# In the second attention, the turns straight behind the scores and the gates parts behind the turns

## The reference, cut to what matters

```python
o_a = diff_attention(qa, ka, va, ...)        # 4 heads, two softmaxes each
o_b = nsa_attention(qb, kvb, ...)            # 8 heads: compressed, selected, window
merged = (jax.nn.sigmoid(gate_a) * (o_a @ w_branch_a[l])
          + jax.nn.sigmoid(gate_b) * (o_b @ w_branch_b[l]))
h = h + merged @ w_out[l]
```

## Time and profile before

| | us |
|---|---|
| median of 3 runs (2418.17 to 2419.32) | 2419.19 |
| the profiled execution | 2417.22 |
| its span, first to last instruction | 2415.5 |
| TensorE busy (97% of the span) | 2351.6 |
| VectorE busy (73%) | 1771.4 |
| ScalarE busy (46%) | 1119.5 |
| GpSimd busy (57%) | 1370.9 |

### The profile page before, as it was taken

How to read it: one execution, slowest core, us unless ns; L and a number is a source line. 1 busy time by engine, 2 the same in 40 slices (tenths; PEclk the granted TensorE clock), 3 DMA queues, 4 the chain that set the end, 5 groups by cost and what they waited for, 6 DMA issues and landing times.

```text
span 2415.5 us, 32822 instructions
## 1 busy us (share of the span) xinstructions
PE 2351.6 (97%) x11991; PEld 1993.6 (83%) x11991; DVE 1771.4 (73%) x2989; ACT 1119.5 (46%) x2163; POOL 1370.9 (57%) x698
## 2 busy tenths in 40 slices
PE   8999999999999999999999999999998999999998
PEld 7866888888886666887889899999998888888887
DVE  4986684253237766655899869999963699999998
ACT  4355322223224555335544368888863333333333
POOL 3423454554432212443535767777777788889885
PEclk9999999999999999999999999999999999999999
DMA  4201222222521111323224578999999799999995
GB/s 160 87 18 37 104 87 91 100 98 84 187 71 54 53 36 36 122 90 107 83 85 156 190 231 310 355 349 353 352 359 396 288 373 376 366 356 366 361 357 211
DMA packets 152500, 476.60 MB, mean 197 GB/s; under 512 B 14768, under 2 KB 47920, under 8 KB 142000
## 3 DMA queue, kind: packets, MB, share of 16 engines
q1 hardware_dynamic: 115504, 340.69, 39.1%
q0 software_dynamic: 36864, 134.23, 15.3%
HBM read 422.44 MB, written 52.43 MB: 197 GB/s over the span
## 4 chain that ended last, share of the span: by engine, by line
PE 87%; DVE 5%; DMA 3%; ACT 2%; POOL 2%; issue 1%; SPq 0%; ACTq 0%; DVEq 0%; POOLq 0%
PE bank_pair L2394 22%; PE bank_pair L286 17%; PE bank_pair L288 17%; PE bank_pair L287 17%; PE bank_pair L2363 2%; DMA u_raw<-expert_u 2%; PE bank_pair L775 1%; PE bank_pair L1448 1%; PE bank_pair L1485 1%; POOL u_lo L2068 1%; PE bank_pair L1501 1%; PE bank_pair L297 1%; PE bank_pair L1457 1%; PE bank_pair L298 1%; DVE stage L2539 1%
## 5 line engine op out<-in xcount | busy, mean ns | idle before, releaser
L255 POOL TENSOR_TENSOR w_lo<-w_raw,w_hi 128x2048 fp32r<-128x2048 f32 (+3 forms) x94 | 408.9, 4350 | 573.2 <-ACT w_hi L250 573.2
L2068 POOL TENSOR_TENSOR u_lo<-u_raw,u_hi 128x1024 fp32r<-128x1024 f32 x128 | 317.9, 2484 | 182.2 <-ACT u_hi L2064 181.5
L286 PE MATMUL bank_pair<-uh,u_lo 128*128 128x384 f32 x1024 | 348.1, 340 | 17.0 <-POOL u_lo L2068 16.5
L288 PE MATMUL bank_pair<-uh,u_hi 128*128 128x384 f32 x1024 | 344.8, 337 | 0.0
L287 PE MATMUL bank_pair<-ul,u_hi 128*128 128x384 f32 x1024 | 344.8, 337 | 0.0
L2124 POOL TENSOR_TENSOR v_lo<-v_raw,v_hi 128x1024 fp32r<-128x1024 f32 x128 | 309.4, 2417 | 43.9 <-ACT v_hi L2120 42.7
L250 ACT ACTIVATE w_hi<-w_raw 128x2048 fp32r<-128x2048 f32 (+3 forms) x95 | 171.5, 1805 | 287.9 <-PE bank_pair L288 280.1
L2588 DVE TENSOR_TENSOR h_raw<-h_raw,g_in 128x384 f32<-128x384 f32 x128 | 272.7, 2131 | 30.7 <-DMA h_raw<-h_scratch 30.7
L2120 ACT ACTIVATE v_hi<-v_raw 128x1024 fp32r<-128x1024 f32 x128 | 135.8, 1061 | 300.3 <-PE bank_pair L2394 243.4
L286 PE MATMUL bank_pair<-xh,w_lo 128*128 128x512 f32 x624 | 245.8, 394 | 5.2 <-DVE sig L1737 2.1
L288 PE MATMUL bank_pair<-xh,w_hi 128*128 128x512 f32 x624 | 243.7, 390 | 0.0
(11 more groups left out here) (458 smaller groups left out, 5226.4 us busy)
## 6 DMA issues: line engine op xcount, KB each, us to landing
w_raw<-w_small SPq DMA_DIRECT2D x77, 1024.0 KB, 4.8
u_raw<-expert_u SPq DMA_DIRECT2D x128, 512.0 KB, 6.1
v_raw<-expert_v SPq DMA_DIRECT2D x128, 512.0 KB, 7.4
h_scratch<-h_act SPq DMA_DIRECT2D x128, 192.0 KB, 4.3
g_scratch<-stage SPq DMA_DIRECT2D x24, 1024.0 KB, 8.8
g_in<-g_scratch SPq DMA_DIRECT2D x16, 1536.0 KB, 11.5
h_raw<-h_scratch SPq DMA_DIRECT2D x128, 192.0 KB, 6.3
w_raw<-w_small SPq DMA_DIRECT2D x8, 768.0 KB, 4.2
```

Source lines behind the costliest of these rows:

```text
L255: pool.tensor_tensor(wl[g % 2][:, :n], raw[g % 2][:, :n], wh[g % 2][:, :n].bitcast(F32), ALU.subtract).then_inc(sem("lo_done"), 1)
L286: pe.matmul(out, al, bh, start=(k == 0), stop=False)
L288: last = pe.matmul(out, ah, bh, start=False, stop=(k == len(pairs) - 1))
L2068: pool.tensor_tensor(u_lo[c % 2][:, :, :], u_raw[c % 4][:, :, :], u_hi[c % 2][:, :, :].bitcast(F32), ALU.subtract)\
```

## The change

Only the order within TensorE's steps changes. The first part of a step no longer stands between the scores and the turns: the turns come straight behind the scores (in steps 1 and 2 the turned compressed weights too), and all parts of the step stand behind the turns and ahead of the values. No instruction, wait or buffer is added or removed, and the streams of the other engines are the same.

```diff
             for s in range(NU + 3):
                 if s < NU:
                     if s >= 2:
                         scores(s)
-                    gates_part(gates_parts(s)[0])
                 if s in (1, 2):
                     compressed_turned(s - 1)
                 if 2 <= s <= NU + 1:
                     transposes(s - 2)
                 if s < NU:
-                    for q in gates_parts(s)[1:]:
+                    for q in gates_parts(s):
                         gates_part(q)
                 if s >= 3:
                     values(s - 3)
```

## The result

The changed kernel takes 2432.13 us (median of 5 runs, 2429.81 to 2436.36) beside 2418.96 of the kernel before on the same chip: ratio 1.0059, 95% interval 1.0045 to 1.0072. The forecast was 2431.3, slower by over 0.2%. The profiled execution, the slowest of the five, took 2436.36, with a span of 2434.6: 19.1 us more than the one before. From L1514 on every line of the new kernel has a number one lower (`weights` ends in L1716 and L1722, `maxima` are L1700 and L1704).

The account below looks back on a forecast made before the run. VectorE was busiest in steps 0 to 16, TensorE full from 816 to 916 us. Terms 2.1 + 0.85 + 3.8 + 5.4 = 12.1 us, added to the median 2419.19, gave 2431.3 us, 0.5% slower, range 2423 to 2436.

Parts of the forecast that it names:

- the signs that were named: Profile after: turns wait on L1254 six times, L1723 some 4 us, other steps' scores-to-scores distance unchanged, TensorE below 100 us.
- The fourth: Sign in the profile after: VectorE's L1723 lasts some 4 us in steps 25, 33 and 41.
- the first steps of the later heads: Steps 24, 28 to 44: turns wait for ScalarE's copy, a part falls behind them; 0.69 and 0.58 alternating, 3.8 us.
- steps 16 to 20: Step 19's turns wait for ScalarE's copy, a part falls behind: 0.69, some 0.15 in step 20; together 0.85 us.
- steps 5, 9 and 13: Turns wait for VectorE's weights, the part now follows them and delays the next scores: 3 x 0.69 = 2.1 us.
- The hold: Steps 25, 33, 41: L1723, now later, waits until POOL's L255 ends, delaying the next turns; 1.8 us each, 5.4.
- The estimate of 0.2 more a time: L1721, ahead of L1723, would be held by POOL too: 0.2 us more per head, 0.6 in all.
- POOL is missed: Rival: L1723 is not held or POOL starts later, only parts behind waiting turns count: 6.7 us, 2425.9; chance 0.20.
- L1705 is caught too: Rival: POOL also holds VectorE's L1705, 3.4 us each instead of 1.8: 16.9 us, 2436.1; chance 0.10.
- The dear switch: Rival: switching between part and turns costs 0.13 us, 32 later steps lose two: 8.3 us back, 2423.0; chance 0.06.
- Covered: Rival: VectorE and ScalarE run ahead elsewhere, only steps 5, 9 and 13 cost: 2.1 us, 2421.3; chance 0.09.
- the first term: Steps 5, 9 and 13, a part behind turns that wait for VectorE's weights: 2.1 us, 0 if VectorE catches up.

Follow-up runs that it names:

- experiment 2: New order from step 16 on, the old one before, against the kernel before: 2431.75 us, ratio 1.0043.
- experiment 4: New order only in steps from 21 on that are not the first of a head, against the kernel before: 2418.17 us, ratio 0.9995.
- experiment 6: New order in steps 24, 32 and 40 alone, against the kernel before: 2425.64 us, ratio 1.0028.
- experiment 1: New order in steps 0 to 15 alone, against the kernel before: 2422.32 us, ratio 1.0009.
- experiment 3: Changed kernel with POOL held until VectorE's weights are done in steps 25, 33 and 41: 2424.19 us, ratio 1.0020 to the kernel before.
- experiment 8: Kernel before with each step's values moved behind the next step's scores, output copies one step later: 2415.58 us, ratio 0.9984.
- experiment 7: Kernel before with only a wait added that starts POOL after VectorE's weights in steps 25, 33 and 41: 2417.45 us, ratio 0.9993.

## Why the prediction was right, and where its steps were off

*The forecast held:* 12.1 us were summed, 13.2 measured, and 11.5 at one clock. TensorE has lost its full 100 us as foreseen, and experiment 2 puts 10.4 of the loss where the sum had 10.1. Of the signs that were named, three came as said: the turns of the six first steps wait for L1254, TensorE is no longer full, and the other steps keep their distance within 0.07 us. The fourth, L1723, came at another instruction.

*A part behind waiting turns.* For the first steps of the later heads, 0.69 and 0.58 were worked out, 3.8 in all; the table has 2.20 + 1.91 = 4.1 in the first profile and 4.2 in the second. For steps 16 to 20 it was 0.85; the table has 0.75. For steps 5, 9 and 13 it was 2.1; the table can't show the first two clean, since a fall of the clock that hit the unchanged steps of experiments 2, 4 and 6 as well (0.94 to 2.45 in the first column) is in it. Step 13 can be read: in experiment 1 the clock is 1.00 from 787 on, and VectorE's wait there has grown by the 0.69 of the sum. At one clock experiment 1 gives 1.0 for all three, give or take 0.9, so 2.1 was on the high side in sum; which of the first two heads paid less stays open.

*The hold.* Time, place and price were right: 1.8 a time forecast, 1.84 to 1.88 measured at full clock. The instruction was not. The sum had L1705 pass by 0.13 us, and it passed by 0.14; but it took L1723 as the one that is caught, because every held row of the trace before was an operation with one input. It was L1721, just ahead of it (L1720 in the new kernel). The Trainium skill (SBUF — State Buffer, Who interferes with whom) says that a VectorE instruction with two SBUF inputs is held by a GpSimd read as well; L1720's 4.42 us beside POOL's 4.53 agrees. The estimate of 0.2 more a time by that page did not come: either instruction is let go at POOL's end (L1720 ends 0.02 us behind it), and the way from there to the turns is the same. The claim "L1723 lasting some 4 us" was therefore wrong, and the end of `weights` right.

*The cover.* The hold was costed without the part that used to stand ahead of the turns of step 26, since the new order takes it away; experiment 6 shows that this is 0.7 of the 1.8. The two halves of the price, a wait that appears and a cover that goes, come from the same moved line.

*The rivals.* That POOL is missed (2425.9) fell with experiments 2 and 3; that L1705 is caught too (2436.1) fell with the rows above, where it lasts 0.17 us. It passed by 0.13 to 0.15 us in each of the three steps, so the forecast was near that rival. The dear switch fell with experiment 4: 0.03 us a step come back, not 0.26. Its 0.13 was no clean price: in step 40 the turns began 0.03 us behind a weight load that had itself waited. The Trainium skill (TensorEngine Tiling (Array Packing), Tiling Modes) says that a change of the tiling mode drains TensorE. Had turning counted as such a change, at 0.13 each, those 21 steps would have given 5.5 us; the trace gives 0.57. "Covered" (2421.3) fell with the 9.5 empty us of TensorE.

*What the sum had no term for* is the clock's 1.5 us, and the 0.7 us that the other steps, in which nothing waits, gave back ("others" in the table, some 0.03 a step), for which it took 0. That the total still came out near is in part luck: the first term, some 1 us on the high side, and this 0.7 stand against the clock.

## What to carry to other kernels

Work that waits for nothing is worth most ahead of the instruction that waits; behind it, its whole length is added to each wait, and in the table that is 0.64 to 0.75 us for a part of 0.69 wherever the turns were late from step 16 on, and nothing where they were not. A delay of under a microsecond can be multiplied when it moves a small instruction past the start of a long one on an engine that holds it: look for the margins (0.13 us here) before adding up lengths. And where an engine waits for scores, moving work that nobody waits for from ahead of them to behind them can pay, as the values in experiment 8 did (2.8 us at one clock).

## What the runs showed beyond that

The granted clock fell behind TensorE's waits, and not in each run. From 764 to 771 us it is 0.76 in all four profiles with the new order in the first 16 steps, and 1.00 in the six without; in the changed kernel the turns there follow an idle 1.14 us:

```profile
765.62 0.55 PE L1457 MATMUL bank_pair<-ident,att_e 128*128 128x128 f32 x3 [1.14 <-DVE att_e L1716]
```

Behind the nine waits of some 1.7 us that the hold makes in three profiles (the changed kernel twice, experiment 2) it fell four times; at the same places of experiments 3 and 6, whose waits there are gone or 0.8 us long, never. From 777 to 787 it fell in eight of the ten profiles, with either order, but not in those of the kernel before and of experiment 7: the profile before showed the first stretch at a better clock than eight of the other nine have it. That the waits cause the falls was not tried by itself; that a step with a fall is 1.5 us longer is in the table.
